# The order around the start of head 1 in a hybrid decoder kernel: state updates ahead of, and the statistics' exchange behind, their old places; near scaling without the wait for far weights

## Chip, cores and metric

The kernel runs on one core of one Trainium2 chip. The metric is the device time of one execution in microseconds (us). Before the change it is 1657.52 us, the median of three runs (1656.7 to 1663.25).

## What is computed

One layer of a decoder trunk on a prompt of 2048 positions and on eight sample sequences of eight positions. After an RMSNorm and one input projection three groups of heads work side by side: A, a dilated sliding-window attention with three branches merged by their softmax denominators; B, a gated linear recurrence after a short convolution; C, the HGRN2 recurrence with a matrix state. An output projection, the residual and a last norm follow. Cut to what the change touches:

```
# group A, prompt: three branches (window, dilation) = (128,1), (512,4), (2048,16)
p = exp(scores - max); l = sum(p); o = p @ v / l; lse = max + log(l)
o_a = sum over branches of softmax(lse) * o          # merged per position and head
# group C, each sample sequence and head, over its 8 tokens
new_state = exp(blast) * state + (k * exp(blast - bcum))^T @ v
```

## The kernel before, in words

There are two blocks. `front` makes the projections and the prompt's recurrences. `attend_project` takes prompt attention, group C of the samples, the sample attention and the output projection. Its order of work is one list written out by `attend_schedule` (and `project_schedule` behind it); each engine's program walks the same list and issues its own part of each step, so the list's order is the order on every queue: TensorE (PE), VectorE (DVE), ScalarE (ACT), GpSimd (POOL) and SyncE (SP, which issues the DMAs).

Prompt attention has six heads, each 32 units: u0 to u31 for head 0, u32 to u63 for head 1, and so on. A unit is 128 queries against the keys of one block row: **far** (strided by 4, `far` = 1) or **near** (the local window). Per unit, PE makes the scores in two products (L2559, L2560), DVE scales, masks and takes the row's extreme in one pass (L2320, "shift"), and ACT exponentiates in place with the row's sum (L2181). PE's unit n waits for DVE's shift of unit n - 3. The narrow units (128 columns) are u32 to u35 and u36; u37 to u43 have 256.

A head's near and far statistics lie in different layouts. When its last unit is exponentiated, step `w` lets DVE spread the far statistics (L2244, `far_stats`); step `x` lets PE bring them into the near layout (L2608) and DVE merge them (`merge`, L2260 to L2271, with ACT's exponential L2184 inside). It writes the near weights (L2270) and then spreads the far weights (L2244, which raises `back_out`). Step `z`: PE brings those back (L2616) and DVE copies them out (L2381, which raises `weights`). Then POOL scales the head's probabilities by the weights: ten passes in the order of `SCALES`, four near, two far, two near, two far (L2096), issued at the head's first `t` step. PE transposes scaled blocks (step `t`, L2627), ACT or DVE copies them out (L1691, L1693), and PE multiplies them with V (step `o`, L2650); these groups run beside the next head's units. The groups of head 0 begin at u42, those of head 5 have no units beside them: they follow `x` and `z` of head 5.

The group-C work of the samples is laid among head 0's and head 1's units. What matters here are the **state updates** `hu`, one per C head, six in all. PE multiplies (L2591, two instructions of 512 columns) what POOL spread by sequence in step `hv` (L2076; its product n waits for PE's update n - 2); DVE multiplies the state by its decay (L2358, both inputs in SBUF) and adds PE's result (L2361, one input in PSUM). From `hu` 2 on PE waits for DVE's update n - 2, since the two share a bank. `hs` stores the state (SP: L1955, L1958). Two query copies of ACT (`qa`, L2143) stand ahead of head 1's first unit. At `lk` SP loads the next head's queries and keys (L1864, L1867), and V and the gates are loaded at L1873, L1875 and L1883. After head 5's last unit the output weights are split by ACT (L2192) and DVE (L2397) beside the last groups.

The old order from u31: u31, w0, u32, u33, x0, u34, hu0, lk2, u35, hu1, hv2, u36, z0, u37, hu2, hv3, u38, hu3, hv4, u39, hu4, hv5, u40, u41, hu5, u42, hs, t0, u43, u44.

Of the kernel before, what the change touches and what calls it, by code (L numbers as in the profile page):

```python
# [40 lines left out]
BASE = 0  # L41
# [1425 lines left out]
def attend_schedule():  # L1467

    units = [(h, i, far, m) for h in range(NH) for i in range(SB) for far in (1, 0) for m in range(NC)]
    groups = []  # L1480
    for h in range(NH):
        rows = [[(i, far, a, j) for i in both for far in range(2) for a in range(NC) for j in block_keys(i, far, a)] for both in LANES]
        blocks = [b for pair in itertools.zip_longest(*rows) for b in pair if b]
        groups += [(h, blocks[b:b + 4]) for b in range(0, len(blocks), 4)]
    per, gper = len(units) // NH, len(groups) // NH
    ends = [max(last_group(groups, h, both[step]) for both in LANES) for h in range(NH) for step in range(2)]
    halves = [(h, j) for j in range(J0, XTILES) for h in ("va", "vb")]
    order, made = [], 0
    for step in ("ha", "va", "vb", "hb", "va", "hp", "qa", "ht", "hc", "vb", "hd", "va", "vb", "hx", "va"):
        order.append(halves.pop(0) if step[0] == "v" else (step, 0))  # L1490
    order.append(("qa", 1))
    hgrn = {0: [("hk", 0), ("he", 0)], 1: [("hz", 0), ("hp", 1)], 2: [("ht", 1), ("hp", 2)], 3: [("ht", 2), ("hp", 3)],
            4: [("ht", 3), ("hj", 0)], 5: [("hj", 1)], 9: [("lk", 1)], 11: [("hq", 0), ("hv", 0)],
            12: [("hr", 0), ("hv", 1)], 13: [("hn", 0)]}
    for h in range(NH):
        hgrn.setdefault(5 + h, []).append(("ho", h))
        if h < NH - 2:
            hgrn.setdefault(6 + h, []).append(("hj", h + 2))
    later = {2: [("hu", 0)], 3: [("hu", 1), ("hv", 2)], 5: [("hu", 2), ("hv", 3)], 6: [("hu", 3), ("hv", 4)],
             7: [("hu", 4), ("hv", 5)], 9: [("hu", 5)], 10: [("hs", 0)]}  # L1500

    def turn():
        nonlocal made
        order.append(("t", made))
        if made >= 2:
            order.append(("o", made - 2))
        if made - 3 in ends:
            order.append(("f", ends.index(made - 3)))
        made += 1

    for u in range(len(units)):
        h, k = u // per, u % per
        order.append(("u", u))
        if h == 0 and k % 2:
            order += hgrn.get(k // 2, [])
            if halves:
                order.append(halves.pop(0))
            if k + 1 == per:
                assert not halves
                order += [("ve", 0), ("qa", 2), ("qa", 3)]  # L1520
        if h == 1:
            order += later.get(k, [])
        if h and h + 1 < NH:
            order += {2: [("lk", h + 1)], 12: [("qn", 2 * h + 2)], 18: [("lv", 1)] * (h == 1), 22: [("qn", 2 * h + 3)]}.get(k, [])
        if h and k in (1, 4):
            order.append(("x" if k == 1 else "z", h - 1))
        if k + 1 == per:
            order.append(("w", h))
        done = u + 1 - per - LEAD
        while done >= 0 and made < done // per * gper + done % per * gper // per + 1:  # L1530
            turn()
    left = (NH - 1) * gper - made
    for n in range(left):
        turn()
        if n in (1, 3):
            order.append(("x" if n == 1 else "z", NH - 1))
    order.append(("pl", 0))
    for n in itertools.count():
        if 4 <= n < 4 + KM:
            order.append(("pw", n - 4))  # L1540
        if n == 11:
            order.append(("pm", 0))
        if n == 16:
            order.append(("pt", 0))
        if made == len(groups):
            break
        turn()
    order += [("o", made - 2), ("o", made - 1), ("f", len(ends) - 1)]
    return units, groups, ends, order + project_schedule()


def attend_project(nc, sem, io, con, zf, zt, zs, mt, mab):
# [4 lines left out]
    units, groups, ends, order = attend_schedule()  # L1557
# [17 lines left out]
    with ExitStack() as ctx:  # L1575
# [146 lines left out]
        hv = lambda h: slice(h * HD, (h + 1) * HD)  # L1722
# [117 lines left out]
        def turned_of(eng, h):  # L1840
            eng.wait_ge(S["turned"], BASE + ends[2 * h + 1] + 1)
# [181 lines left out]
        def _(pool):  # L2023
# [25 lines left out]
            for kind, n in order:  # L2049
                if kind == "hd":  # L2050
# [6 lines left out]
                    for m, l in enumerate(LV):  # L2057
                        hs = HALVES[l]
# [4 lines left out]
                elif kind == "qn":  # L2063
                    h = n // 2
                    pool.wait_ge(q_in[h % 2], BASE + 32 * (h // 2 + 1))
                    pool.wait_ge(S["scores"], BASE + PER * (h - 1))
                    tiles, src = near_queries(n)
                    G.tensor_copy(tiles, src).then_inc(S["q_near"], 1)
                elif kind == "hv":
                    if n == 0:  # L2070
                        pool.wait_ge(H["pairs"], BASE + 1 + len(LV))
                        pool.wait_ge(H["v_in"], BASE + 32)
                        pool.wait_ge(H["const"], BASE + hgrn_const)
                    if n >= 2:
                        pool.wait_ge(H["us"], BASE + n - 1)
                    G.tensor_tensor(h_vb[n % 2][:], h_vv[:, hv(n)].unsqueeze(1).to_broadcast([NS, NB, HD]),  # L2076
                                    h_rowm[:].unsqueeze(2).to_broadcast([NS, NB, HD]), ALU.mult).then_inc(H["vb_r"], 1)
                elif kind == "hr":
                    pool.wait_ge(H["stat"], BASE + 2)
                    G.tensor_tensor(h_small[:, 2, :], h_small[:, 1, :], con["mhalf"][:NS, 0:1].to_broadcast([NS, NH]),  # L2080
                                    ALU.pow).then_inc(H["scaled"], 1)
                elif kind == "t":
                    h = groups[n][0]
                    if n and groups[n - 1][0] == h:
                        continue
                    pool.wait_ge(S["weights"], BASE + h + 1)
                    for far, i, part in SCALES:
                        if far:
                            p, m0 = pfs[h % 2][i][:], 0
                        elif i == 0:  # L2090
                            p, m0 = ((pna[h % 2][:, 0:1, 0:P], 0), (pna[h % 2][:, 1:2, :], 1), (pnb[h % 2][:, 0:2, :], 2))[part]
                        else:
                            p, m0 = pnb[h % 2][:, NC * i - 2:NC * (i + 1) - 2, :], 0
                        _, ms, w = p.shape
                        by_row = wt[h % 2][:, far, :].rearrange("p (m i) -> p m i", i=SB)[:, m0:m0 + ms, i]
                        G.tensor_tensor(p, p, by_row.unsqueeze(2).to_broadcast([P, ms, w]), ALU.mult).then_inc(S["scaled"], 1)  # L2096
                elif kind == "si":
                    turned_of(pool, NH - 1)
                    used_of(pool, NH - 1)
                    final_of(pool, NH - 1)  # L2100
                    G.iota(tcol[:, 0:1], pattern=[[0, 1]], base=0, channel_multiplier=1).then_inc(Z["made"], 1)
                    G.memset(qbd[:], 0.0).then_inc(Z["made"], 1)
                    G.iota(dist[:, 0, 0:NEAR], pattern=[[-1, NJ], [-NJ, P]], base=NEAR, channel_multiplier=0).then_inc(Z["made"], 1)
                    G.iota(dist[:, 0, NEAR:NW], pattern=[[-1, NT]], base=0, channel_multiplier=0).then_inc(Z["made"], 1)
                    G.memset(smask[:, NW:NK], 0.0).then_inc(Z["made"], 1)
                    G.memset(orow[:], 0.0).then_inc(Z["made"], 1)
                    G.memset(far_rows[:], 0.0).then_inc(Z["made"], 1)
                elif kind == "sr":
                    pool.wait_ge(Z["k_in"], BASE + KLOADS * (n + 1))
                    read(pool, "Q", n)  # L2110
                    G.tensor_tensor(kk[:, 0:FJ, :], kk[:, 0:FJ, :], qrep[:].unsqueeze(1).to_broadcast([P, FJ, AW]),
                                    ALU.mult).then_inc(Z["product"], 1)
                elif kind == "pg":
                    s = small[n % 2][:rows_of(n)]
                    pool.wait_ge(Z["mean"], BASE + n + 1)
                    G.tensor_tensor(s[:, 2:3], s[:, 1:2], con["mhalf"][:rows_of(n), 0:1], ALU.pow).then_inc(Z["rstd"], 1)  # L2116
# [699 lines left out]
```

## Time and profile before

| | |
|---|---|
| median of three runs | 1657.52 us |
| profiled execution | 1662.47 us, its span 1660.4 us |
| mean granted clock of TensorE | 0.974 of full speed |
| busy: PE, PE weight loads, DVE, ACT, POOL | 95%, 81%, 59%, 50%, 38% of the span |
| HBM | 106 GB/s over the span |

One execution was profiled; times within it are us from the span's start. Busy shares are over the whole span, which has stages with different limits. The granted clock is a share of full speed (1.00 is 2.4 GHz, 0.50 is 1.2 GHz). In the rows below, L12 is line 12 of the kernel, and `out<-in` names what an instruction writes and reads.

### The profile page before, as it was taken

To read this page: it belongs to the slowest core of one execution; us is meant where nothing else is said; L and a number is where in the kernel's file an instruction comes from. 1 tells how busy PE (TensorE), PEld (TensorE's weight loads), DVE (VectorE), ACT (ScalarE), POOL (GpSimd) and SP (SyncE) were. 2 spreads that over 40 slices of the span, in tenths; PEclk is the share of its full clock that TensorE was granted. 3 is DMA by queue.
4 is the path that set the end of the run, shared out by engine and by line. 5 is a ranking of instruction groups with operands and counts; after the bars stand their busy time and mean duration, and the time that the engine had idled before them with its cause. 6 is when DMAs were issued, how large, how long until landed. Compare 5 with 4: busy or idle time off the path is not lost. (4 is left out here: it accounts for less than half of the span.)

```text
span 1660.4 us, 38525 instructions
## 1 busy us (share of the span) xinstructions
PE 1577.6 (95%) x15345; PEld 1338.0 (81%) x15345; DVE 979.3 (59%) x2066; ACT 823.4 (50%) x1603; POOL 628.0 (38%) x754
## 2 busy tenths in 40 slices
PE   7999999999999999999999998799999898999997
PEld 6988989999887888888788887796777576777775
DVE  4436665433577777677777765326666557555652
ACT  5427877122455555667767664435777521211210
POOL 1102221100566666666666663306456502121110
PEclk9999999999999999999999998997999899999999
DMA  6310012145212121221211211648992374866651
GB/s 236 101 60 29 22 46 69 59 127 147 77 42 74 44 75 42 53 62 27 67 32 42 58 27 50 160 105 189 248 223 53 100 238 141 272 199 209 205 171 42
DMA packets 196287, 175.27 MB, mean 106 GB/s; under 512 B 84915, under 2 KB 180686, under 8 KB 193806
## 3 DMA queue, kind: packets, MB, share of 16 engines
q1 hardware_dynamic: 196110, 172.82, 36.5%
q8 instruction: 122, 2.00, 0.5%
q14 instruction: 55, 0.45, 0.1%
HBM read 123.18 MB, written 52.84 MB: 106 GB/s over the span
## 5 line engine op out<-in xcount | busy, mean ns | idle before, releaser
L49 PE MATMUL f_bank<-c_ht,c_whi 128*128 128x384 f32 (+1 forms) x864 | 320.1, 371 | 0.0
L51 PE MATMUL f_bank<-c_ht,c_wlo 128*128 128x384 f32 (+1 forms) x864 | 302.1, 350 | 0.0
L50 PE MATMUL f_bank<-c_ht,c_whi 128*128 128x384 f32 (+1 forms) x864 | 301.5, 349 | 0.0
L854 ACT ACTIVATE f_scr<-f_scr 128x384 f32<-128x384 f32 (+1 forms) x210 | 114.0, 544 | 205.8 <-POOL f_scr L627 205.8
L1068 DVE TENSOR_TENSOR f_scr<-f_scr 128x192 f32<-128x192 f32 (+1 forms) x210 | 105.4, 502 | 139.3 <-ACT f_scr L854 138.7
L49 PEld LDWEIGHTS f_bank<-c_ht,c_whi 128*128 128x128 f32 x864 | 162.2, 188 | 15.4 <-issue 1.4
L50 PEld LDWEIGHTS f_bank<-c_ht,c_whi 128*128 128x128 f32 x864 | 162.6, 188 | 9.7 <-issue 1.4
L51 PEld LDWEIGHTS f_bank<-c_ht,c_wlo 128*128 128x128 f32 x864 | 162.2, 188 | 9.0
L626 POOL TENSOR_TENSOR f_scr<-f_scr 128x192 f32<-128x192 f32 (+1 forms) x210 | 134.1, 639 | 43.3 <-PE f_tps L1254 40.6
L1059 DVE COPY_PREDICATED f_scr<-f_scr,f_tps 128x384 f32<-128x384 int32 (+1 forms) x210 | 130.3, 621 | 18.4 <-PE f_tps L1254 10.2
L49 PE MATMUL a_s<-a_whi,a_mhi 128*128 128x512 f32 (+1 forms) x306 | 125.8, 411 | 4.7 <-DVE a_y L2485 4.7
L50 PE MATMUL a_s<-a_wlo,a_mhi 128*128 128x512 f32 (+1 forms) x306 | 122.4, 400 | 0.0
L652 POOL TENSOR_SCALAR f_scr<-f_scr,c_lbl 128x384 f32<-128x384 f32 (+1 forms) x30 | 43.2, 1442 | 202.7 <-ACT f_scr L820 202.7
L1254 PEld LDWEIGHTS f_tps<-f_scr 128*32 128x32 f32 (+1 forms) x5184 | 75.0, 113 | 40.0 <-issue 30.0
L1254 PE MATMUL f_tps<-f_scr 128*32 128x32 f32 (+1 forms) x5184 | 96.3, 200 | 2.3 <-DVE f_scr L1068 2.3
L2116 POOL TENSOR_TENSOR a_small<-a_small,c_mhalf 128x1 f32<-128x1 f32 (+1 forms) x17 | 9.2, 542 | 234.5 <-DVE a_small L2489 234.5
L49 PE MATMUL f_bank<-c_whi,c_ht 128*128 128x384 f32 x256 | 91.0, 355 | 4.6 <-DVE c_wlo L909 2.8
L51 PE MATMUL f_bank<-c_whi,c_ht 128*128 128x384 f32 x256 | 87.4, 341 | 0.0
L50 PE MATMUL f_bank<-c_wlo,c_ht 128*128 128x384 f32 x256 | 87.4, 341 | 0.0
L49 PE MATMUL f_bank<-c_htail,c_whi 128*128 128x448 f32 x216 | 83.8, 388 | 0.0
L51 PE MATMUL a_s<-a_whi,a_mlo_a 128*128 128x512 f32 (+1 forms) x204 | 82.0, 402 | 0.0
L51 PE MATMUL f_bank<-c_htail,c_wlo 128*128 128x448 f32 x216 | 79.2, 367 | 0.0
(405 smaller groups left out, 3806.1 us busy)
## 6 DMA issues: line engine op xcount, KB each, us to landing
f_wraw<-in_w_in SPq DMA_DIRECT2D x27, 512.0 KB, 4.1
zs<-f_stage SPq DMA_DIRECT2D x48, 192.0 KB, 2.4
a_k<-in_ck SPq DMA_DIRECT2D x48, 192.0 KB, 5.5
a_v<-in_cv SPq DMA_DIRECT2D x48, 192.0 KB
f_scr<-in_xp SPq DMA_DIRECT2D x16, 512.0 KB, 4.4
a_x<-in_xp SPq DMA_DIRECT2D x16, 512.0 KB, 5.4
out_y_prompt<-a_y SPq DMA_DIRECT2D x16, 512.0 KB, 2.9
zt<-f_stage SPq DMA_DIRECT2D x38, 192.0 KB, 1.9
```

What stands on the lines that cost most here:

```text
L49: nc.tensor.matmul(out, w_hi, m_hi, start=start, stop=False)
L50: nc.tensor.matmul(out, w_hi, m_lo, start=False, stop=False)
L51: return nc.tensor.matmul(out, w_lo, m_hi, start=False, stop=stop)
L626: G.tensor_tensor(d[:, :, hs:], b[:, :, hs:], r, ALU.subtract)
L652: G.tensor_scalar(key[:, :n], key[:, :n], lbl[:, 1, h:h + 1], None, ALU.mult).then_inc(S["gated"], 1)
L854: A(lev[i % 3][:, :n], lev[i % 3][:, :n], ACT.Exp).then_inc(S["expd"], 1)
L1059: V.copy_predicated(attn[:, :n].rearrange("p (j t) -> p j t", t=P), m.bitcast(I32).unsqueeze(1).to_broadcast([P, nt, P]), lp[x % 2][:, :n] ...
L1068: V.tensor_tensor(e[:, :, hs:], e[:, :, hs:], q[:, :, hs:], ALU.mult).then_inc(S["xlev"], 1)
L1254: mm = nc.tensor.matmul(lp[x % 2][k0:k0 + w, queries], left[:, keys], right[:, queries], start=True, stop=True)
L2116: G.tensor_tensor(s[:, 2:3], s[:, 1:2], con["mhalf"][:rows_of(n), 0:1], ALU.pow).then_inc(Z["rstd"], 1)
```

## The change

Three edits. In head 1 (units u32 to u63, k counts from 0) the updates `hu` stand one or two units earlier, with the POOL products between them, and `hs` one unit earlier. The exchange of head 0's statistics, `x` and `z`, stands one unit later (after k = 2 and k = 5 instead of 1 and 4); that of the other heads stays. POOL waits for `back_out` (the near weights are ready) ahead of a head's scaling, and for `weights` (the far weights are back) only ahead of each far pass.

```
-    later = {2: [("hu", 0)], 3: [("hu", 1), ("hv", 2)], 5: [("hu", 2), ("hv", 3)], 6: [("hu", 3), ("hv", 4)],
-             7: [("hu", 4), ("hv", 5)], 9: [("hu", 5)], 10: [("hs", 0)]}
+    later = {0: [("hu", 0)], 1: [("hu", 1), ("hv", 2)], 3: [("hu", 2), ("hv", 3)], 4: [("hu", 3), ("hv", 4)],
+             6: [("hu", 4), ("hv", 5)], 8: [("hu", 5)], 9: [("hs", 0)]}
...
-        if h and k in (1, 4):
-            order.append(("x" if k == 1 else "z", h - 1))
+        merged, spread = (2, 5) if h == 1 else (1, 4)
+        if h and k in (merged, spread):
+            order.append(("x" if k == merged else "z", h - 1))
...
-                    pool.wait_ge(S["weights"], BASE + h + 1)
+                    pool.wait_ge(S["back_out"], BASE + h + 1)
                     for far, i, part in SCALES:
                         if far:
+                            pool.wait_ge(S["weights"], BASE + h + 1)
                             p, m0 = pfs[h % 2][i][:], 0
```

The new order from u31: u31, w0, u32, hu0, u33, hu1, hv2, u34, lk2, x0, u35, hu2, hv3, u36, hu3, hv4, u37, z0, u38, hu4, hv5, u39, u40, hu5, u41, hs, u42, t0, u43, u44.

## Rows read from the trace of the kernel before

**Rows 1.** The page, part 1: busy us (share) of each engine

```profile
PE 1577.6 (95%) x15345; PEld 1338.0 (81%) x15345; DVE 979.3 (59%) x2066; ACT 823.4 (50%) x1603; POOL 628.0 (38%) x754
```

**Rows 2.** Stretches: from:to, us, busy of each engine, granted clock, DMA share, GB/s

```profile
1131.00:1135.00 4.00, 3.34 (x17) 1.54 (x18) 2.13 (x12) 2.97 (x9) 1.05 (x2) 0.94 0.55 162
1135.00:1146.00 11.00, 9.44 (x24) 3.96 (x25) 9.90 (x27) 3.22 (x12) 5.44 (x6) 0.50 1.09 242
...
1155.00:1172.00 17.00, 17.00 (x149) 13.19 (x146) 10.62 (x36) 13.04 (x38) 8.60 (x5) 1.00 0.89 205
```

**Rows 3.** Instructions in order of time, DVE: first operation of the merges of heads 0 to 2

```profile
1131.98 0.18 DVE L2260 TENSOR_TENSOR a_mix<-a_sn,a_x 128x16 f32<-128x16 f32 x1
...
1173.88 0.18 DVE L2260 TENSOR_TENSOR a_mix<-a_sn,a_x 128x16 f32<-128x16 f32 x1
...
1205.97 0.18 DVE L2260 TENSOR_TENSOR a_mix<-a_sn,a_x 128x16 f32<-128x16 f32 x1
```

**Rows 4.** In order of time, DVE: start, us, instruction, [idle before, releaser]

```profile
1131.22 0.29 DVE L2244 TENSOR_TENSOR a_exch<-a_sf,a_quarter 128x128 f32<-128x128 f32 x1 [0.82 <-ACT a_pnb L2181]
1134.00 0.50 DVE L2264 TENSOR_TENSOR a_mix<-a_sn,a_mix 128x16 f32<-128x16 f32 x1 [1.53 <-ACT a_mix L2184]
...
1136.58 0.69 DVE L2358 TENSOR_TENSOR a_h_s<-a_h_s,a_h_gl 128x512 f32<-128x512 f32 x1
1137.30 0.69 DVE L2361 TENSOR_TENSOR a_h_s<-a_h_s,a_t 128x512 f32<-128x512 f32 x1
...
1144.19 1.35 DVE L2358 TENSOR_TENSOR a_h_s<-a_h_s,a_h_gl 128x512 f32<-128x512 f32 x1
1147.35 1.51 DVE L2358 TENSOR_TENSOR a_h_s<-a_h_s,a_h_gl 128x512 f32<-128x512 f32 x1
```

**Rows 5.** In order of time, PE: x0, update 0, z0, update 2, unit 44

```profile
1131.66 0.27 PE L2608 MATMUL a_x<-a_exch,a_unit_row 128*32 128x32 f32 x8 [1.11 <-DVE a_exch L2244]
1132.22 1.12 PE L2591 MATMUL a_t<-a_h_vb,a_h_kdt 64*128 64x512 f32 x2
1136.45 0.31 PE L2616 MATMUL a_x<-a_exch,a_unit_row 128*32 128x16 f32 x8 [0.93 <-DVE a_exch L2244]
1138.13 2.04 PE L2591 MATMUL a_t<-a_h_vb,a_h_kdt 64*128 64x512 f32 x2 [0.62 <-DVE a_h_s L2361]
1151.15 0.41 PE L2559 MATMUL a_s<-a_khi,a_qn 128*128 128x256 f32 x1
```

**Rows 6.** In order of time, POOL: scaling of head 0, first four passes and two later

```profile
1143.98 0.96 POOL L2096 TENSOR_TENSOR a_pna<-a_pna,a_wt 128x128 f32<-128x128 f32 x2
1144.91 3.39 POOL L2096 TENSOR_TENSOR a_pnb<-a_pnb,a_wt 128x512 f32<-128x512 f32 x2
...
1151.59 3.75 POOL L2096 TENSOR_TENSOR a_pnb<-a_pnb,a_wt 128x1024 f32<-128x1024 f32 x2
```

**Rows 7.** In order of time, SP, and landing of the loads of V

```profile
1138.72 1.03 SPq L1875 DMA_DIRECT2D a_vf<-zt  x1
DMA to landing us min/median/max: 3.4/6.1/8.0
```

**Rows 8.** Waits from 1155 to 1300: us in total, times, longest

```profile
POOL a_pna L2096 <- DVE a_wt L2381: 27.5, 2, 13.7
...
PE a_t L2627 <- ACT a_pt L1691: 0.7, 2, 0.3
```

**Rows 9.** In order of time: the last head's merge (first and last operation), scaling, transposes

```profile
1301.88 0.18 DVE L2260 TENSOR_TENSOR a_mix<-a_sn,a_x 128x16 f32<-128x16 f32 x1 [0.85 <-PE a_x L2608]
...
1303.74 0.22 DVE L2244 TENSOR_TENSOR a_exch<-a_mix,a_quarter 128x64 f32<-128x64 f32 x1
1304.73 0.97 POOL L2096 TENSOR_TENSOR a_pna<-a_pna,a_wt 128x128 f32<-128x128 f32 x2 [14.12 <-DVE a_wt L2381]
1308.62 0.47 PE L2627 MATMUL a_t<-c_ident,a_pna 128*128 128x128 f32 x1 [2.03 <-POOL a_pnb L2096]
1324.23 0.45 PE L2627 MATMUL a_t<-c_ident,a_pnb 128*128 128x128 f32 x1 [5.84 <-DVE a_pt L1693]
```

## The prediction

> **What bounds the kernel now.** First the page: TensorE is busy 95% of the span [rows 1] and its granted clock is 0.974 of full in the mean, so what counts is where it isn't. A table of stretches around head 1's start shows it [rows 2]: the granted clock is 0.94 from 1131 to 1135, 0.50 (1.2 GHz) from 1135 on, and 1.00 (2.4 GHz) from 1155 to 1172 (it falls at 1134.5 and rises at 1155.0), and from 1155 on PE is busy in all of every stretch. The moved steps lie in the slow part. Merge to merge, head 1's units take 1173.88 - 1131.98 = 41.9 us, head 2's 32.1 us [rows 3].
>
> Next the instructions of that part. DVE spreads head 0's far statistics at 1131.22 [rows 4]; PE had then been without work for 1.11 us [rows 5]. DVE's merge then waits 1.53 us for ScalarE's exponential, which stands behind two query copies on its queue [rows 4]. PE's z0 waits 0.93 us for the merge's result, and only then come the six state updates [rows 5]. An update costs PE 1.1 us at full clock and 2.0 us at half [rows 5]; DVE 0.72 us to the addition's start and 0.60 more, 1.3 us [rows 4]. DVE's last addition, 0.69 us, follows the decay product that ends at 1148.86 [rows 4], and PE reaches unit 44 at 1151.15 [rows 5]. I measure the change at that point: behind it PE is full to the end of the heads, so a shift there reaches the end undiminished.
>
> **Part 1, the order.** Nothing is added: the same twelve PE products, twelve DVE passes, six POOL products. From 1129.4 the new order gives PE u32, hu0, u33, hu1, u34, x0, u35, hu2, u36, hu3, u37, z0, u38, hu4, u39, u40, hu5, u41, u42, t0, u43, u44.
>
> PE: hu0 and hu1 need nothing from head 0's statistics, so 2 x 1.1 us fill the old hole; x0 comes at about 1132.7 instead of 1131.66, u35 at 1133.1. hu2 needs the first update finished (they share a bank): about 1133.3.
> DVE: spread 1131.22; u32; update 0 until 1133.2; u33; update 1 until 1134.8; u34; merge from 1135.0. ScalarE's copies are over by then, so the 1.53 us wait becomes about 0.3, as in head 5 (merge 1301.88 to 1303.96, 2.1 us [rows 9]). Two POOL products fall beside it; one held a merge operation before (0.50 us, its like at 1131.98 took 0.18 [rows 3, 4]), so I add 0.7 for two: the merge's result at about 1138, 1.6 us later than before. This is the price: z0 and, behind it in PE's queue, u38 and hu4 wait; PE stands about 1 us at 1137.
> From there: DVE's whole work from 1131.22 to unit 41 is spread 0.2, five narrow shifts of 0.24 and four of 0.34 (2.6), six updates (7.9), merge 2.1, copy 0.1: 12.9, plus 0.7. It would end at 1144.8.
>
> What is late next is the lock between DVE and POOL. POOL's scaling for t0 started at 1143.98, directly behind its last update product [rows 6]; now that product follows hu3, and scaling starts at about 1138.2, under updates 2 to 5. In before, the two decay products under it took 1.35 and 1.51 us against 0.69: +0.66 and +0.82 [rows 4]. Four of these make 3.0 us: DVE reaches u41 at 1147.8, and after its shift (0.34) and PE's u43 PE takes u44 at 1148.6. PE's own sum agrees: hu4 waits for update 2 until 1140.5, 2.0; u39, u40; hu5 from 1143.7, 2.0; u41, u42, t0 (0.9), u43: 1148.3. So the gain is 1151.15 - 1148.6 = 2.5 us. Bounds: with no lock waits PE's half-clock sum still gives 1147.4, 3.7 us; with each wait through the running POOL pass and the whole next (0.95 + 1.89, from the two passes of 3.75 us together [rows 6]) it is 4 x 2.84 = 11.4 on 1144.8, so 1156.6: 5.4 us slower. I take 0.75 a wait, the two rows of the same operation.
>
> The Trainium skill (SBUF — State Buffer, SBUF: two separate sides) calls this port pair an exclusive lock held for the whole instruction; it speaks against the change. The trace agrees: the decay product of 1147.35 ends 0.56 us behind POOL's pass that ends at 1148.30 [rows 4, 6].
>
> The clock: I take it as still lost at 1134.5 or one step later. PE is fuller until 1137 but stands for z0, then for update 2; and in before it stayed at 0.50 through 1135 to 1146 with PE busy 9.44 of 11 us [rows 2].
>
> SP: hs stands one unit earlier, so its two stores (of which nothing on the chip waits but the loads of the next V, for head 2) are issued with the last update, a little earlier: zero. lk2 now stands ahead of x0, but SP has no x step: zero. V for the first outputs was issued by 1139.75 and lands in at most 8.0 us, 1147.8 [rows 7], before t0 either way.
>
> **Part 2, POOL's wait.** Near scaling starts with the merge's result instead of the copied far weights. From 1155 to 1300 POOL idles ahead of its scaling, 13.7 us at the longest of two waits for the weights, and the list of waits there has none of PE for POOL; its smallest is 0.7 us [rows 8]: zero. Four more waits per head, one a far pass, are added, on a value long reached. Queued behind them are only the query copies. In head 5 PE does wait, 2.03 us until 1308.62, for the fourth near pass, which runs from 1304.73 without a gap; the merge's result was there at 1303.96, 0.77 us before POOL began [rows 9]. Less the 0.08 us of a wake-up, 0.7 us. It carries on: the next stall of PE, 5.84 us until 1324.23 [rows 9], is for a copy of DVE that stands behind weight splits with two SBUF inputs, which the lock makes wait for POOL's last passes. Bounds: 0 if something else ends that stall, 1.0 with the faster clock around 1308.
>
> **Sum.** 2.5 + 0.7 = 3.2 us. The profiled execution took 1662.47 (span 1660.4), 4.95 above the median of 1657.52; its stretches are taken as the median's: 1657.5 - 3.2 = **1654.3 us** (a like execution 1659.3).
>
> **Rivals.**
> Clock kept: the denser PE from 1130 to 1137 keeps 2.4 GHz. Then DVE still reaches u41 at 1147.8 and PE u44 by 1148.3, and what ran at half clock behind u44 (3.8 us, 1151.15 to 1155) takes 1.9: 2.8 + 1.9 + 0.7 = 5.4, so 1652.1; with no lock waits 3 us less. For it: only 1.1 us of hole made way for it. Against: the stretch goes at DVE's pace, and the six updates are 6.7 us of PE at full clock (6 x 1.12 [rows 5]) in DVE's 16.6. The Trainium skill (TensorE: Matmul & The Clock Gate, What's actually happening) says the throttled state is the default and activity releases it; that is this case.
> Lock: POOL's scaling takes the place of the wait for z0. Price as bounded: 5.4 slower less 0.7, 1662.2. It decides from 1.6 us per decay product on (6.4 / 4), twice what rows 4 show; for it, POOL's 1.89 us passes [rows 6] are the ones that now meet updates 3 to 5.
> Absorbed: the shift is lost before 1155, because t0 or o0 wait for scaling or V as late as before; then only 0.7: 1656.8. Against: V is there and scaling starts 6 us earlier.
> The change does nothing at all: not possible, the queues are in program order.
>
> **Numbers.** Forecast 0.56, clock kept 0.19, lock 0.10, absorbed 0.15. About 0.5% (8.3 us) is what a measurement of this kernel can tell from no change. The forecast's own bounds give 1652.8 to 1657; clock kept reaches to 1649 and is cut at 1650; the lock case is taken in up to 1659.5, over a third of its way. Range 1650 to 1659.5. Faster by over 0.5% needs below 1649.2: clock kept together with no lock waits and a second slow stretch lost, 0.07. Slower by over 0.5% needs above 1665.8: 0.03. Else 0.90.
>
> **What would show it.** Right: PE without the 1.11 us wait ahead of x0; the merge's ACT wait near 0.3; back_out's spread near 1138; decay products 2 to 5 at 1.2 to 1.6 us; POOL scaling from about 1138; granted clock still 0.50 from about 1135 or 1138 to 1151.6 or 1155; from the spread at 1131.22 to head 1's merge 40.2 us instead of 42.7; head 5's scaling 0.1 us behind the merge's spread instead of behind the weights' copy. Wrong: no 0.50 stretch around 1140 (clock kept); decay products over 1.6 us (lock); those 42.7 us unchanged (absorbed).

## The result, and the profile after

The changed kernel takes 1669.34 us in the median of twelve runs, the kernel before 1659.86 us in the median of twelve beside it: ratio 1.0048, 95% interval 1.0035 to 1.0060. Most of the changed kernel's runs lie between 1669 and 1672 us, three at 1665 to 1666 and one at 1659. The forecast was 3.2 us faster and its range ended at 1659.5; the change costs 9.5 us by the medians and 8.0 us (5.8 to 10.0) by the ratio. The kernel before is 2.3 us slower over these twelve runs than over the three that the forecast started from (1657.52), so that much of the distance between 1654.3 and 1669.34 is not the change.

The page of the profiled execution (1669.14 us, span 1667.2 us, mean granted clock 0.972) hardly tells why, part 1 against [rows 1]:

```profile
PE 1575.8 (95%) x15345; PEld 1336.6 (80%) x15345; DVE 991.5 (59%) x2066; ACT 823.8 (49%) x1603; POOL 630.6 (38%) x754
```

One figure moved: DVE is "busy" 12.2 us longer with the same 2066 instructions. The stretches around head 1's start say where (columns as in [rows 2]: from:to, us, busy PE, PEld, DVE, ACT, POOL, granted clock, DMA share, GB/s):

```profile
1129.00:1135.00 6.00, 5.41 (x30) 3.36 (x29) 3.87 (x12) 4.56 (x13) 2.52 (x2) 0.94 0.83 220
1135.00:1146.00 11.00, 11.00 (x27) 4.21 (x25) 10.39 (x29) 2.77 (x12) 7.82 (x7) 0.50 1.00 215
1146.00:1155.00 9.00, 1.28 (x4) 0.91 (x4) 9.00 (x6) 1.09 (x4) 9.00 (x5) 0.50 1.02 228
1155.00:1165.00 10.00, 5.34 (x28) 4.85 (x28) 6.77 (x14) 4.67 (x15) 5.56 (x4) 0.50 0.96 217
1165.00:1175.00 10.00, 10.00 (x86) 7.87 (x85) 5.52 (x21) 6.99 (x22) 0.00 (x0) 1.00 0.88 201
```

Until 1146 the new order does what it was to do: PE is busy in all 11 us, against 9.44 before [rows 2]. Then it works 1.28 of 9 us, while DVE and POOL are both shown as busy in all of them. DVE in order of time:

```profile
1131.88 0.93 DVE L2246 TENSOR_TENSOR a_exch<-a_sf,a_quarter 128x128 f32<-128x128 f32 x1 [0.81 <-ACT a_pnb L2183]
...
1132.93 0.68 DVE L2360 TENSOR_TENSOR a_h_s<-a_h_s,a_h_gl 128x512 f32<-128x512 f32 x1
...
1136.77 0.91 DVE L2266 TENSOR_TENSOR a_mix<-a_sn,a_mix 128x16 f32<-128x16 f32 x1 [0.30 <-ACT a_mix L2186]
...
1138.58 0.22 DVE L2246 TENSOR_TENSOR a_exch<-a_mix,a_quarter 128x64 f32<-128x64 f32 x1
...
1138.99 0.69 DVE L2360 TENSOR_TENSOR a_h_s<-a_h_s,a_h_gl 128x512 f32<-128x512 f32 x1
...
1140.52 1.53 DVE L2360 TENSOR_TENSOR a_h_s<-a_h_s,a_h_gl 128x512 f32<-128x512 f32 x1
...
1143.04 0.17 DVE L2383 COPY a_wt<-a_x 128x16 f32<-128x16 f32 x1
...
1143.46 1.91 DVE L2360 TENSOR_TENSOR a_h_s<-a_h_s,a_h_gl 128x512 f32<-128x512 f32 x1
...
1146.69 11.98 DVE L2360 TENSOR_TENSOR a_h_s<-a_h_s,a_h_gl 128x512 f32<-128x512 f32 x1
1158.71 0.69 DVE L2363 TENSOR_TENSOR a_h_s<-a_h_s,a_t 128x512 f32<-128x512 f32 x1
```

and POOL beside it:

```profile
1139.22 1.35 POOL L2077 TENSOR_TENSOR a_h_vb<-a_h_vv,a_h_rowm 64x512 f32<-64x512 f32 x1 [1.58 <-PE a_t L2593]
1140.54 0.96 POOL L2098 TENSOR_TENSOR a_pna<-a_pna,a_wt 128x128 f32<-128x128 f32 x2
1141.47 3.35 POOL L2098 TENSOR_TENSOR a_pnb<-a_pnb,a_wt 128x512 f32<-128x512 f32 x2
1144.78 3.36 POOL L2098 TENSOR_TENSOR a_pf<-a_pf,a_wt 128x512 f32<-128x512 f32 x2
1148.10 3.75 POOL L2098 TENSOR_TENSOR a_pnb<-a_pnb,a_wt 128x1024 f32<-128x1024 f32 x2
1151.82 6.32 POOL L2098 TENSOR_TENSOR a_pf<-a_pf,a_wt 128x2048 f32<-128x2048 f32 x2
1158.09 2.48 POOL L2069 CAST a_qn<-a_qst 128x1024 fp32r<-128x1024 f32 x2
```

The sixth decay product (both inputs in SBUF) takes 0.69 us when alone. Here it is issued at 1146.69, under a pass of POOL, and ends at 1158.67, 0.53 us behind the end of POOL's tenth and last pass (1151.82 + 6.32 = 1158.14). It waited out the running pass, POOL's sixth, and the four behind it. POOL's queue doesn't end there: two casts of queries follow without a gap, and DVE got in ahead of them (they take 2.48 us here and 2.02 where nothing disturbs them, as in x3 below). The three such products under the scaling take 1.53, 1.91 and 11.98 us: 13.35 us over their 0.69. PE's rows for the same stretch (u44 is the last one; it stood at 1151.15 in [rows 5]):

```profile
1130.41 1.12 PE L2593 MATMUL a_t<-a_h_vb,a_h_kdt 64*128 64x512 f32 x2
...
1133.25 0.27 PE L2610 MATMUL a_x<-a_exch,a_unit_row 128*32 128x32 f32 x8
...
1134.48 2.04 PE L2593 MATMUL a_t<-a_h_vb,a_h_kdt 64*128 64x512 f32 x2 [0.59 <-DVE a_h_s L2363]
...
1139.79 0.31 PE L2618 MATMUL a_x<-a_exch,a_unit_row 128*32 128x16 f32 x8
...
1159.66 0.45 PE L2629 MATMUL a_t<-c_ident,a_pna 128*128 128x128 f32 x1 [12.38 <-DVE a_h_s L2363]
...
1160.97 0.41 PE L2561 MATMUL a_s<-a_khi,a_qn 128*128 128x256 f32 x1
```

The hole ahead of x0 is gone, z0 doesn't wait, and then one hole of 12.38 us stands ahead of t0. From unit 32 to unit 44 PE needs 30.8 us where it needed 21.7. Those 9.2 us are the whole loss in the profile; the time from head 1's merge to head 2's is unchanged (1215.89 - 1183.80 = 32.09 us, against 1205.97 - 1173.88 = 32.09 in [rows 3]):

```profile
1183.80 0.17 DVE L2262 TENSOR_TENSOR a_mix<-a_sn,a_x 128x16 f32<-128x16 f32 x1
...
1215.89 0.18 DVE L2262 TENSOR_TENSOR a_mix<-a_sn,a_x 128x16 f32<-128x16 f32 x1
```

The half-clock stretch is 30.7 us long (1134.3 to 1165.0) instead of 20.5, but what is longer lies in PE's wait for DVE: behind u44 both kernels have about 4 us of it left.

The last head shows part 2, to be read against [rows 9]:

```profile
1310.66 0.29 DVE L2246 TENSOR_TENSOR a_exch<-a_sf,a_quarter 128x128 f32<-128x128 f32 x1 [0.67 <-ACT a_pnb L2183]
...
1313.98 0.97 POOL L2098 TENSOR_TENSOR a_pna<-a_pna,a_wt 128x128 f32<-128x128 f32 x2 [14.82 <-DVE a_exch L2246]
...
1317.87 0.33 PE L2629 MATMUL a_t<-c_ident,a_pna 128*128 128x128 f32 x1 [1.35 <-POOL a_pnb L2098]
...
1330.77 0.45 PE L2629 MATMUL a_t<-c_ident,a_pnb 128*128 128x128 f32 x1 [4.62 <-DVE a_pt L1694]
```

POOL is released by the merge's spread now, and PE's wait for the fourth pass falls from 2.03 to 1.35 us.

### The profile page after: what moved, and what is told of

Same layout as the page of the kernel before. It is cut to its first block and busy times, and to the rows that moved or that the text cites. A ratio compares the mean times of both kernels' runs of the same rounds, so it can differ in the third digit from the quotient of the medians.

```text
span 1667.2 us, 38525 instructions
## 1 busy us (share of the span) xinstructions
PE 1575.8 (95%) x15345; PEld 1336.6 (80%) x15345; DVE 991.5 (59%) x2066; ACT 823.8 (49%) x1603; POOL 630.6 (38%) x754
## 5 line engine op out<-in xcount | busy, mean ns | idle before, releaser
L1059 DVE COPY_PREDICATED f_scr<-f_scr,f_tps 128x384 f32<-128x384 int32 (+1 forms) x210 | 130.4, 621 | 18.3 <-PE f_tps L1254 10.1
```

The lines of the kernel that those rows point to most:

```text
L1059: V.copy_predicated(attn[:, :n].rearrange("p (j t) -> p j t", t=P), m.bitcast(I32).unsqueeze(1).to_broadcast([P, nt, P]), lp[x % 2][:, :n] ...
```

## The experiments

**The theories.** The lock (L): the loss is DVE's wait for POOL, and it needs both parts, the order that brings updates 3 to 5 up to the scaling and the wait that starts the scaling earlier. The order (O): the order by itself costs, whatever POOL does. The clock (K): the longer half-clock stretch is the cause and not a consequence. Later ones were on what lets DVE in again: a hole between two of POOL's passes (S), or a short pass that comes next (T). Ratios are to the kernel before, measured beside each kernel, with their 95% interval. From unit 32 to unit 44 on PE is the reading that each profile gives without the noise of the whole: 21.7 us before, 30.8 after.

**1. The order alone** (x1_order_only; run once more as x15_order_again). The new order, with POOL's wait as it was:

```
-                    pool.wait_ge(S["back_out"], BASE + h + 1)
+                    pool.wait_ge(S["weights"], BASE + h + 1)
                     for far, i, part in SCALES:
                         if far:
-                            pool.wait_ge(S["weights"], BASE + h + 1)
```

> The new order of updates, x0 and z0 (part 1) alone; POOL waits for the weights ahead of all passes, as before. Theory L (the lock: POOL's early start put its passes under the updates' decay products): scaling of head 0 starts with the weights' copy, about 2.7 us later than in the changed kernel (1143.2 instead of 1140.5), the last decay product meets a short pass at most twice and takes 1 to 3 us, not 12; ratio to before 0.997 to 1.001. Theory O (the order itself costs, because the updates hold DVE and the merge comes late): as slow as the changed kernel, 1.004 to 1.006. Theory K (a longer stretch at half clock is the cause, the lock an effect of nothing): also 1.004 or more, with the half-clock stretch of some 30 us.

> The new order alone once more: its first ratio, 0.9993 with an interval of 0.0015 to each side, was less than its 3.3 us at head 1's start (0.998). If those 3.3 us reach the end, 0.997 to 0.9985; if they are given back later, 0.999 to 1.000 again.

Unit 32 to 44 is 18.4 us in both, 3.3 less than before. Ratio 0.9993 (0.9978 to 1.0007), and 0.9977 (0.9964 to 0.9989) the second time: not slower, the second time a little faster. DVE and POOL in order of time:

```profile
1140.82 0.77 DVE L2359 TENSOR_TENSOR a_h_s<-a_h_s,a_h_gl 128x512 f32<-128x512 f32 x1
...
1142.92 0.70 DVE L2359 TENSOR_TENSOR a_h_s<-a_h_s,a_h_gl 128x512 f32<-128x512 f32 x1
```

```profile
1140.64 1.42 POOL L2097 TENSOR_TENSOR a_pna<-a_pna,a_wt 128x128 f32<-128x128 f32 x2 [1.86 <-DVE a_wt L2382]
1142.03 3.35 POOL L2097 TENSOR_TENSOR a_pnb<-a_pnb,a_wt 128x512 f32<-128x512 f32 x2
```

Released by the copied weights, POOL starts 12.3 us behind unit 32 instead of 10.4. The last two decay products get in at the first boundary between passes that they meet, 0.77 and 0.70 us, and it is the passes they meet that stretch (1.42 and 3.35 us; undisturbed pairs take 0.96 and 2.90, as in x3). The order theory falls.

**2. The wait alone** (x2_wait_only). The kernel before with the new waits of POOL:

```
-                    pool.wait_ge(S["weights"], BASE + h + 1)
+                    pool.wait_ge(S["back_out"], BASE + h + 1)
                     for far, i, part in SCALES:
                         if far:
+                            pool.wait_ge(S["weights"], BASE + h + 1)
```

> POOL's earlier wait (part 2) alone, in the old order. In the old order POOL's last update product, not the weights, released head 0's scaling, so nothing moves at head 1's start. Theory L: head 0 as before, and at the end of the heads the 0.7 us of part 2: ratio 0.999 to 1.000. Theory O: the same. If part 2 costs by itself (four more waits a head), ratio 1.001 or more.

Ratio 0.9997 (0.9985 to 1.0009). Unit 32 to 44 is 21.6 us, the decay products are those of [rows 4] (the last two 1.35 and 1.52 us): in the old order the last group-C product of POOL holds the scaling back, not the weights. Neither part alone costs anything, so the loss is in the two together.

**3. The same update without an operation that takes the lock** (x3_fused). DVE's product and addition become eight operations with one input in PSUM; PE's, ACT's and POOL's programs are as in the changed kernel:

```
-                    V.tensor_tensor(h_s[:, :, hv(n)], h_s[:, :, hv(n)], decay, ALU.mult).then_inc(H["s_tmp"], 1)
...
-                    V.tensor_tensor(h_s[:, :, hv(n)], h_s[:, :, hv(n)], bank_h("U", n)[:].rearrange("p (b v) -> p b v", v=HD),
-                                    ALU.add).then_inc(H["s_new"], 1)
+                    for b in range(NB):
+                        ins = V.scalar_tensor_tensor(out=h_s[:, b, hv(n)], in0=h_s[:, b, hv(n)], scalar=h_gl[:, b * NH + n:b * NH + n + 1],
+                                                     in1=bank_h("U", n)[:, b * HD:(b + 1) * HD], op0=ALU.mult, op1=ALU.add)
+                    ins.then_inc(H["s_new"], 1)
```

> The changed kernel, but DVE's update is eight fused operations with one SBUF and one PSUM input (state times decay plus product) instead of a decay product with two SBUF inputs and an addition. Theory L: these don't wait for POOL; no operation of the updates takes over 0.5 us, head 1's start loses its 12 us wait, and the kernel is faster than before: ratio 0.995 to 0.999. Theories O and K: the order still costs, ratio 1.002 or more.

Ratio 0.9986 (0.9971 to 1.0000), unit 32 to 44 19.4 us. The first update, before any pass of the scaling, and the last, in the middle of them (they start as early as in the changed kernel, 10.3 us behind unit 32), take the same time:

```profile
1133.02 1.61 DVE L2361 SCALAR_TENSOR_TENSOR a_h_s<-a_h_s,a_h_gl,a_t 128x64 f32<-128x64 f32 x8
...
1146.40 1.62 DVE L2361 SCALAR_TENSOR_TENSOR a_h_s<-a_h_s,a_h_gl,a_t 128x64 f32<-128x64 f32 x8 [0.77 <-PE a_t L2592]
```

Same order, same early scaling, no wait, and no loss against the kernel before: DVE's wait goes with its second SBUF input. The trace shows no ports. The Trainium skill (SBUF — State Buffer, SBUF: two separate sides) has the pair of ports that DVE and POOL share as an exclusive lock for the whole instruction, the other side fully blocked. These traces agree: 11.98 us for a product with two SBUF inputs, no wait in eight operations with one.

**4. POOL held back until the updates are through** (x4_hold). The changed kernel and, ahead of head 0's passes:

```
+                    if h == 0:
+                        pool.wait_ge(H["s_tmp"], BASE + NH)
```

> The changed kernel, but POOL's scaling of head 0 also waits until all six decay products are done. Theory L: no decay product takes over 1.1 us; scaling starts about 1147 instead of 1140.5, and the first transposes wait for it until about 1151, as before the change: ratio 0.998 to 1.001. Theories O and K: ratio 1.003 or more.

All six decay products take 0.68 to 0.69 us; ratio 0.9985 (0.9973 to 0.9997), unit 32 to 44 20.5 us. The scaling starts 15.3 us behind unit 32, where the expectation had about 17 (1147 less 1130.14). Now PE waits for POOL:

```profile
1143.61 0.97 POOL L2100 TENSOR_TENSOR a_pna<-a_pna,a_wt 128x128 f32<-128x128 f32 x2 [4.89 <-DVE a_h_s L2362]
```

```profile
1147.49 0.47 PE L2631 MATMUL a_t<-c_ident,a_pna 128*128 128x128 f32 x1 [2.21 <-POOL a_pnb L2100]
```

So there is a too late as well: t0 needs four passes, and the 2.21 us that it waits are what this order gives away against x1's 18.4.

**5. The changed kernel once more** (x10_again), for how firm the twelve microseconds are:

> The changed kernel once more, for a second profile of it. Theory S or L with a repeating timing: the last decay product again waits 8 us or more and the time is over 1665 us. If the 12 us wait was one execution's chance: it takes under 4 us and the time is near 1660 us.

1668.2 us in its one run, against 1660.43 in the median before. DVE, the last decay product:

```profile
1145.70 11.98 DVE L2360 TENSOR_TENSOR a_h_s<-a_h_s,a_h_gl 128x512 f32<-128x512 f32 x1
```

In this second execution the six products repeat to 0.01 us (0.68, 0.69, 0.69, 1.53, 1.91, 11.98), so this is no accident of a single one. That every execution has the long wait isn't shown: four of the twelve runs of the changed kernel were some 3 to 10 us faster than most of the others, and none of these was profiled.

**6. A hole behind every pass** (x7_gaps). POOL's early start as in the change, but in head 0 each pass waits for the one before it to have finished:

```
-                    for far, i, part in SCALES:
+                    for step, (far, i, part) in enumerate(SCALES):
+                        if h == 0 and step:
+                            pool.wait_ge(S["scaled"], BASE + step)
```

> The changed kernel, but in head 0 each of POOL's ten passes waits for the one before it to have ended, so that POOL's queue has a hole between passes. Theory S (a waiting DVE operation gets in at the end of a pass only if the next pass isn't there yet; back to back passes shut it out): no decay product waits longer than one pass, at most 2.6 us, and the 12 us wait is gone: ratio 0.998 to 1.000. Theory R (who gets in at a pass's end is by chance of phase, the hole changes nothing): some decay product still takes over 4 us and the ratio is 1.003 or more.

Ratio 0.9967 (0.9951 to 0.9983), better than expected; unit 32 to 44 18.3 us. DVE's last two decay products:

```profile
1142.92 1.21 DVE L2362 TENSOR_TENSOR a_h_s<-a_h_s,a_h_gl 128x512 f32<-128x512 f32 x1
...
1145.45 0.98 DVE L2362 TENSOR_TENSOR a_h_s<-a_h_s,a_h_gl 128x512 f32<-128x512 f32 x1
```

and the passes around them:

```profile
1142.54 3.35 POOL L2100 TENSOR_TENSOR a_pnb<-a_pnb,a_wt 128x512 f32<-128x512 f32 x2
1145.96 3.36 POOL L2100 TENSOR_TENSOR a_pf<-a_pf,a_wt 128x512 f32<-128x512 f32 x2
```

The pair that starts at 1142.54 ends at 1145.89, the next starts at 1145.96; without the wait the pairs follow on the end of the one before or a little ahead of it (1141.47 + 3.35 = 1144.82 in the changed kernel, the next at 1144.78). With holes of 0.07 us the last product takes 0.98 us instead of 11.98 and waits only for what is left of the running pass. One thing here isn't the work of a hole at its own place: the fourth product (1140.83) takes 0.69 us instead of 1.53. It got in ahead of the first pass, where there is no hole (the first two passes take 1.61 us together instead of 0.96); it was issued 0.05 us before POOL's product of group C ended, which is where it lost in the changed kernel (1140.52 and 1140.57).

**7. Head 0 keeps its old wait, the other heads have the new one** (x8_split_wait; run once more as x14_split_again):

```
-                    pool.wait_ge(S["back_out"], BASE + h + 1)
+                    pool.wait_ge(S["back_out" if h else "weights"], BASE + h + 1)
```

> The changed kernel, but in head 0 POOL waits for the weights ahead of all passes; heads 1 to 5 keep the earlier wait. Theory L: head 1's start as in the run with the order alone (unit 32 to unit 44 in 18.4 us instead of 21.7) and the last head's scaling 0.7 us earlier: ratio 0.996 to 0.999, faster than both kernels. If the parts don't add up, 0.999 to 1.001.

> The best version so far again (new order; head 0's scaling waits for the weights, heads 1 to 5 start it with the merge's result), beside the order alone on one chip. Theory L: unit 32 to unit 44 in about 18.2 us, no decay product over 1 us, ratio to before 0.995 to 0.998, and some 0.7 us (0.0004) below the order alone, less than these rounds can tell.

Ratio 0.9957 (0.9939 to 0.9976) and 0.9962 (0.9946 to 0.9979), 1653.15 and 1655.48 us against 1660.43 and 1659.8: it beats both kernels. The profiles account for about 4 us of it (3.3 to 3.5 at unit 44, 0.7 at the last head, so 0.9975, near the top of both intervals); where the rest comes from isn't shown. Beside it, the order alone had 1656.46 us (x15), 1.0 us more, which the intervals don't tell apart. Unit 32 to 44 is 18.1 and 18.4 us, and the last head's start is that of the change. Its stretches:

```profile
1135.00:1145.00 10.00, 10.00 (x26) 4.13 (x24) 9.39 (x34) 3.59 (x14) 5.32 (x6) 0.50 0.98 216
1145.00:1155.00 10.00, 9.92 (x56) 8.17 (x56) 5.09 (x20) 6.18 (x21) 10.00 (x6) 0.66 1.04 229
1155.00:1165.00 10.00, 10.00 (x89) 7.52 (x88) 5.51 (x21) 8.02 (x23) 6.66 (x4) 1.00 1.09 244
```

PE is full through all three, and still at half clock until about 1152 (0.66 in the mean of ten us is 6.8 us at 0.50 and 3.2 at 1.00): the half-clock stretch is 17.1 us here. This denser order didn't keep the clock; the slow stretch ended 3.4 us earlier. The clock theory falls too: everything from update 2 to unit 44 is at 0.50 before and after, behind unit 44 the two have 3.9 and 4.0 us of half clock left (1151.15 to 1155.0, 1160.97 to 1165.0), and in x3, x7 and x8, where DVE isn't shut out, the stretch is 17.1 us.

**8. Who gets in at a boundary without a hole.** Two kernels asked. One has a single hole, ahead of the seventh pass (x12_one_gap), the other cuts head 0's last five passes into halves without holes (x13_halves):

```
+                        if h == 0 and step == 6:
+                            pool.wait_ge(S["scaled"], BASE + step)
```

```
+                        if h == 0 and step >= 5:
+                            half = ms // 2
+                            G.tensor_tensor(p[:, 0:half], p[:, 0:half], by_row[:, 0:half].unsqueeze(2).to_broadcast([P, half, w]), ALU.mult)
+                            G.tensor_tensor(p[:, half:ms], p[:, half:ms], by_row[:, half:ms].unsqueeze(2).to_broadcast([P, half, w]), ALU.mult).then_inc(S["scaled"], 1)
+                            continue
```

> The changed kernel with one hole only: POOL waits for the end of head 0's sixth pass ahead of its seventh, the first boundary at which the last decay product lost in both profiles. Theory S (a waiting DVE operation gets in where the next pass isn't yet there): the last decay product ends about 0.6 us behind the sixth pass, so takes 2.0 us instead of 12; the rest as in the changed kernel; unit 32 to unit 44 in 20 to 21 us instead of 30.8; ratio 0.997 to 1.000. Theory R (the hole does nothing by itself, shorter total pressure does): it still takes over 4 us, ratio 1.003 or more.

> The changed kernel, but from the sixth pass of head 0 on each of POOL's passes is issued as two halves, back to back and without a hole (passes of 512 columns for the sixth to eighth). All three boundaries that DVE won in the profiles had a pass of 512 columns behind them, and four of those that it lost one of 1024 or more. Theory T (it gets in where the next pass is short): the last decay product takes at most 1.7 us; ratio 0.997 to 1.000. If the length of the next pass doesn't matter: it waits through several halves, over 4 us, ratio 1.003 or more.

The halves: the last wait falls to 1.13 us, in at the first boundary between halves, and the others stay at 1.53 and 1.91; unit 32 to 44 is 20.0 us. The ratio is 1.0003 (0.9990 to 1.0015), just outside what was expected; the 1.7 us that the profile shows at unit 44 would be 0.9990, the edge of the interval, and whether they reach the end is open. The single hole: ratio 0.9991 (0.9977 to 1.0005), unit 32 to 44 22.8 us, an expectation missed, and the rows show a wait that nobody had expected, in DVE's third decay product:

```profile
1137.44 5.05 DVE L2362 TENSOR_TENSOR a_h_s<-a_h_s,a_h_gl 128x512 f32<-128x512 f32 x1
...
1148.17 0.98 DVE L2362 TENSOR_TENSOR a_h_s<-a_h_s,a_h_gl 128x512 f32<-128x512 f32 x1
```

```profile
1138.12 0.96 POOL L2100 TENSOR_TENSOR a_pna<-a_pna,a_wt 128x128 f32<-128x128 f32 x2
1139.05 2.89 POOL L2100 TENSOR_TENSOR a_pnb<-a_pnb,a_wt 128x512 f32<-128x512 f32 x2
1145.25 3.35 POOL L2100 TENSOR_TENSOR a_pf<-a_pf,a_wt 128x512 f32<-128x512 f32 x2 [3.31 <-DVE a_wt L2385]
```

Here POOL got to the scaling 0.9 us earlier by its distance from unit 32 (9.5 instead of 10.4), so the queue of four near passes met update 2. DVE's product was issued at 1137.44, under POOL's last group-C product, and waited through it and all four passes until POOL stopped for the far weights at 1141.94; it ended at 1142.49, 0.55 us behind. The last product (1148.17) got in at the planned hole. Wherever a waiting product met a hole it got in: twice in x7, twice here and twice in the kernel of the next experiment, so nothing contradicts S. But a hole isn't needed: the halves had none, and the last product got in at its first boundary. That the hole and not a shifted phase (theory R) let it in is therefore likely and not proven. T fails: in x12 DVE was shut out at four boundaries though the passes behind the first three were short ones (0.39, 0.60 and 1.03 us), and in x1 the product of 0.70 us got in ahead of a pass of 1024 columns. In the changed kernel DVE got in at three boundaries without a hole (the ends of the waits of 1.53, 1.91 and 11.98 us, the last ahead of the casts) and at six others not. What decides there stays open.

**9. Holes in the last head too** (x11_gaps_ends). x8 with holes behind the passes of heads 0 and 5:

```
+                        if h in (0, NH - 1) and step:
+                            pool.wait_ge(S["scaled"], BASE + len(SCALES) * h + step)
```

> Head 0's scaling waits for the weights, heads 1 to 5 keep the earlier wait, and in head 0 and head 5 each of POOL's passes waits for the one before it. At head 1's start the holes find nothing left to shorten (decay products 0.7 us already). At the end DVE's first weight splits took 3.0 to 4.6 us each under POOL's last passes where 1.2 us is usual, but never longer than the running pass, so by theory S holes win nothing there: ratio 0.995 to 0.998, as without them. If back to back passes cost at the end too: 0.5 us or more below the kernel without holes, at 0.993 to 0.995.

Ratio 0.9976 (0.9966 to 0.9986). Nothing is won in the last head, rather lost: PE waits 1.71 us for the fourth pass instead of 1.35, and then 5.10 instead of 4.62 for DVE:

```profile
1301.60 0.33 PE L2631 MATMUL a_t<-c_ident,a_pna 128*128 128x128 f32 x1 [1.71 <-POOL a_pnb L2100]
...
1315.00 0.45 PE L2631 MATMUL a_t<-c_ident,a_pnb 128*128 128x128 f32 x1 [5.10 <-DVE a_pt L1694]
```

The readings together, all from the profiles:

| kernel | unit 32 to 44, us | scaling of head 0 starts behind unit 32, us | decay products 2 to 5, us | half-clock stretch, us | ratio |
|---|---|---|---|---|---|
| before | 21.7 | 14.5 | 0.69, 0.69, 1.35, 1.51 | 20.5 | 1 |
| after | 30.8 | 10.4 | 0.69, 1.53, 1.91, 11.98 | 30.7 | 1.0048 |
| x10 the change again | 30.8 | 10.4 | 0.69, 1.53, 1.91, 11.98 | 30.7 | one run |
| x1 order alone | 18.4 | 12.3 | 0.69, 0.68, 0.77, 0.70 | 17.1 | 0.9993, 0.9977 |
| x2 wait alone | 21.6 | 14.4 | 0.69, 0.69, 1.35, 1.52 | 20.5 | 0.9997 |
| x3 fused | 19.4 | 10.3 | eight of 0.27 per update | 17.1 | 0.9986 |
| x4 POOL held | 20.5 | 15.3 | 0.69, 0.69, 0.69, 0.69 | 20.5 | 0.9985 |
| x7 holes | 18.3 | 10.4 | 0.69, 0.69, 1.21, 0.98 | 17.1 | 0.9967 |
| x8 split wait (and x14) | 18.1, 18.4 | 12.0, 12.3 | 0.69, 0.69, 0.77, 0.69 | 17.1 | 0.9957, 0.9962 |
| x12 one hole | 22.8 | 9.5 | 5.05, 0.69, 1.42, 0.98 | 20.5 | 0.9991 |
| x13 halves | 20.0 | 10.4 | 0.69, 1.53, 1.91, 1.13 | 20.5 | 1.0003 |
| x11 split wait, holes | 18.5 | 12.3 | 0.69, 0.69, 0.77, 0.81 | 17.1 | 0.9976 |

## Why the prediction was wrong, point by point

**The step that failed** is in part 1: "Four of these make 3.0 us ... I take 0.75 a wait, the two rows of the same operation". It priced the wait of an operation with two SBUF inputs by two that had gone well. Measured, update 2 didn't wait at all, and the other three waited 0.84, 1.22 and 11.29 us, 13.35 in all instead of 3.0. The short waits and the long one don't differ in what the prediction looked at: the second of its two rows (issued at 1147.35) stood under the fourth pass, with six more to follow without a hole, and got in at the first boundary; so did the 1.91 us one of the changed kernel. The last one stood under the sixth pass, with four to follow, and lost at each. The step took a small wait as a property of the operation. With the order alone unit 44 comes 3.3 us earlier than before, and the waits put 12.4 us on top (30.8 against 18.4 us): but for rounding, the 9.2 us.

**The bound** failed with it: "the running POOL pass and the whole next", 2.84 us a wait, was no bound, because a waiting product can lose at one boundary after the other as long as the next pass follows without a gap. No run shows what bounds the wait; the long one ended with the last pass, but at a boundary like the others, since POOL's casts followed at once. Had the prediction taken the end of the scaling as a bound (ten passes, in the changed kernel 17.6 us from their start, 1158.14 - 1140.54), the slower side would have been worth far more than 5.4 us. The sums around it are also uneven: from unit 41 to unit 44 the forecast takes 0.8 us (1147.8 to 1148.6), the bound 0.4 (1156.2 to 1156.6) and the 6.4 us of the rival none (1151.15 - 1144.8). With 0.8 throughout the bound is 5.9 us slower (1157.0) and the rival decides from 1.4 us a wait; neither comes near what was measured.

**The rival "Lock"** had the mechanism, the place (update products 3 to 5 under POOL's passes) and a point of decision that was passed: 1.6 us of wait per product, 6.4 in all, against 13.35. (The signs then name 1.6 us as the product's whole time; by that reading, too, two of the three are over it.) It got 0.10, and its price came from the same bound. Its time was 1662.2, 4.7 us slower than the start of 1657.5; measured is 9.5 us slower.

**The order** was right, and better than forecast. Ahead of the lock every sign stood: no wait ahead of x0, 0.30 us for the exponential instead of 1.53, two products of POOL beside DVE's small operations (0.93 and 0.91 us for work of 0.29 and 0.18), the merge's spread at 1138.58, where 1138 plus the 0.7 us by which this execution runs late was predicted. x1, which is part 1 alone, gains 3.3 us at unit 44, where the sum said 2.5; two decay waits were nearly nothing (0.08 and 0.01 us), since the scaling starts late in x1. The price named for the order, PE standing 1 us for z0, wasn't there: when the merge's spread ended at 1138.80 PE was still busy with update 3 at half clock, and z0 follows at 1139.79 without a wait.

**The start of the scaling** was missed by 1.7 us: 1138.2 was predicted (1138.9 with this execution's lateness), 1140.54 measured. POOL's last group-C product waited for PE's update 3 (1.58 us, then 1.35 of its own, itself over its 1.04 elsewhere). Part 2 has no price in head 0 in the prediction, but it has an effect there: with the old wait the weights' copy at 1143.04 would have been what releases POOL in the new order, as in x1 and x8, and the new wait is what took this protection away. The prediction costed POOL's new wait only behind 1155 (zero, and 0.7 us in head 5), and booked under the order a scaling start (1138.2) that only the new wait allows, so what the two do together stood nowhere as a price of its own.

**Part 2 at the end** was right to the tenth. From the last spread of statistics to the end of PE's second long stall it is 20.8 us in x1 (1316.76 - 1295.96) and 20.1 in x2 and in the changed kernel (1330.77 - 1310.66): 0.7 us. In the profiled execution of before that distance was 23.5 us (1324.23 - 1300.73), 2.7 more than in x1, which has the same wait: the granted clock of that execution was 0.86 from 1305 to 1310 and 0.80 from 1310 to 1315, and 1.00 in x1 and in the changed kernel at the same work. The 5.84 us stall was its own (4.6 in x1), and the prediction took it for the kernel's. This is also why the profiled executions differ by only 6.7 us and the medians by 9.5. Heads 1 to 4 lose nothing by part 2, as forecast: from merge to merge they take 32.09, 31.7, 32.1 and 32.1 us before and after.

**The clock** was right: half clock until after u44 in every kernel, and 3.4 us less of it where the order works (17.1 against 20.5 us). "Clock kept" didn't come about; "absorbed" neither, since x1 has its gain still at unit 64 (38.6 us from unit 32 instead of 42.2).

**What stays open**: by what DVE gets in at some boundaries between two POOL operations that follow without a hole and not at others, and so what a wait of this kind is to be priced at. The first ratio of the order alone, 0.9993, is weaker than the 3.3 us of its profile (0.998), though its interval holds that; the second, 0.9977, agrees.

## What to carry to other kernels

Before moving a DVE operation with two SBUF inputs, or starting a run of POOL operations earlier, lay both queues beside each other: an operation that comes under an unbroken queue of POOL can wait up to a pass of it (at most 1.22 us here) or far longer (4.36 us in x12, 11.29 us in the changed kernel, to the end of the scaling), and nothing in the rows of before told which. A forecast needs both prices. Two parts of a change that are harmless apart are to be costed once more together, each in the order that the other makes. If they must overlap, let POOL wait for its own last pass now and then (0.07 us a time; in each of six cases DVE got in), give DVE's operation an input in PSUM, or start the POOL queue when the last such operation is nearly through, and no later than its reader allows.

## What the runs showed of the hardware that was not expected

- A DVE operation with two SBUF inputs was shut out through five POOL passes in a row, 11.98 us for 0.69 us of work, and the same to 0.01 us in a second execution; another through five of POOL's operations, 5.05 us.
- Each of the six times that a waiting product met a hole between POOL's operations (five of 0.07 to 0.08 us, one of 3.31 us) it got in. Without a hole it sometimes did and sometimes didn't, in two cases with the same 0.05 us between its issue and the end of POOL's operation (x7 and the changed kernel).
- In the profile such a wait is counted as DVE's busy time, not as idle: it stands in no list of waits, what stands there is PE's 12.38 us behind it. The sign is one instruction far longer than its like.
